# Keys' inverse norms, low-rank and weighing products, and the low halves at a seam of the expert passes

## The reference, cut to what matters

```
p    = h @ w_in                          # f, v/g, nine feature tiles (rw), then q, k, v of the window attention
kk   = k * kk_scale ; kk = kk / max(norm(kk over the 64 of a head), 1e-12)
w, a = sigmoid(w0 + w_up(tanh(..))), sigmoid(a0 + a_up(..))     # "low-rank", two directions
out  = scores @ v  for the gated linear attention, rms-normed and gated         # "weighing"
```

## Time and profile before

| | |
|---|---|
| median of 3 runs | 2022.44 us (2021.68 to 2023.82) |
| time of the profiled execution | 2018.09 us |
| its span, first to last instruction | 2016.3 us |
| mean granted clock of TensorE | 0.97 |
| TensorE busy | 1830.6 us, 91% |
| VectorE busy | 1610.4 us, 80% |
| ScalarE busy | 1090.9 us, 54% |
| GpSimd busy | 145.0 us, 7% |

### The profile page before, as it was taken

One profiled execution on the slowest core, in us unless ns is written; L12 is line 12 of the kernel. 1 busy time (PEld: TensorE's weight loads), 2 busy tenths in 40 slices (PEclk: granted clock), 3 DMA queues, 4 the chain that ended last, 5 costly groups with the idle time before them and its releaser, 6 DMA issues. The chain is left out here.

```text
span 2016.3 us, 31666 instructions
## 1 busy us (share of the span) xinstructions
PE 1830.6 (91%) x12866; PEld 1562.5 (77%) x12866; DVE 1610.4 (80%) x2113; ACT 1090.9 (54%) x1316; POOL 145.0 (7%) x151
## 2 busy tenths in 40 slices
PE   2989989998989989999899968997999999999998
PEld 2876769997866769997777657876788788787886
DVE  6778888987788888987579487557888888988887
ACT  2643636653653637562565333125677677776775
POOL 0000000000000000000056047300000000000000
PEclk9989999999999999999999987998899999999999
DMA  7667766656567757556522100006599899898997
GB/s 282 208 222 242 256 226 252 233 205 225 198 217 244 260 189 289 219 196 242 182 83 64 61 12 15 19 16 247 191 372 375 316 377 375 318 373 316 349 381 292
DMA packets 158288, 460.54 MB, mean 228 GB/s; under 512 B 11072, under 2 KB 13760, under 8 KB 155584
## 3 DMA queue, kind: packets, MB, share of 16 engines
q1 hardware_dynamic: 158144, 458.52, 63.7%
HBM read 457.43 MB, written 1.05 MB: 227 GB/s over the span
## 5 line engine op out<-in xcount | busy, mean ns | idle before, releaser
L217 DVE TENSOR_TENSOR me_wlow<-me_w,me_whigh 128x2048 fp32r<-128x2048 f32 (+1 forms) x203 | 451.5, 2247 | 77.5 <-ACT me_whigh L212 77.1
L212 ACT ACTIVATE me_whigh<-me_w 128x2048 fp32r<-128x2048 f32 (+1 forms) x203 | 380.3, 1885 | 116.9 <-PE ps L225 107.2
L223 PE MATMUL ps<-me_whigh,me_xhigh 128*128 128x512 f32 x512 | 204.0, 398 | 5.1 <-PEq L124 3.1
L225 PE MATMUL ps<-me_whigh,me_xlow 128*128 128x512 f32 x528 | 206.9, 392 | 0.0
L223 PE MATMUL ps<-up_xhigh,ffn_whigh 128*128 128x256 f32 x704 | 199.8, 284 | 2.6 <-DVE ffn_wlow L217 1.5
L224 PE MATMUL ps<-me_wlow,me_xhigh 128*128 128x512 f32 x512 | 200.5, 392 | 0.0
L224 PE MATMUL ps<-up_xlow,ffn_whigh 128*128 128x256 f32 x704 | 199.2, 283 | 0.0
L225 PE MATMUL ps<-up_xhigh,ffn_wlow 128*128 128x256 f32 x704 | 199.2, 283 | 0.0
L217 DVE TENSOR_TENSOR ffn_wlow<-ffn_w,ffn_whigh 128x2048 fp32r<-128x2048 f32 (+1 forms) x72 | 149.3, 2110 | 42.4 <-ACT ffn_whigh L212 42.3
L217 DVE TENSOR_TENSOR mix_wlow<-mix_w,mix_whigh 128x1024 fp32r<-128x1024 f32 (+2 forms) x116 | 140.0, 1210 | 21.8 <-ACT mix_whigh L212 21.7
L212 ACT ACTIVATE ffn_whigh<-ffn_w 128x2048 fp32r<-128x2048 f32 (+1 forms) x72 | 123.2, 1760 | 43.1 <-PE ps L225 43.1
(11 more groups left out here) (682 smaller groups left out, 4147.8 us busy)
## 6 DMA issues: line engine op xcount, KB each, us to landing
me_w<-w_exp_gate SPq DMA_DIRECT2D x34, 2048.0 KB, 9.8
me_w<-w_exp_up SPq DMA_DIRECT2D x34, 2048.0 KB, 10.3
me_w<-w_exp_down SPq DMA_DIRECT2D x32, 2048.0 KB, 10.4
mix_w<-w_mix SPq DMA_DIRECT2D x108, 512.0 KB, 4.0
mix_ada_w<-ada_w SPq DMA_DIRECT2D x96, 512.0 KB, 4.6
ffn_w<-ffn_w_up SPq DMA_DIRECT2D x20, 2048.0 KB, 7.8
ffn_w<-ffn_w_down SPq DMA_DIRECT2D x8, 2048.0 KB, 8.8
sec_w<-w_in SPq DMA_DIRECT2D x31, 512.0 KB, 3.6
```

Of the source, the lines that this page charges most:

```text
L212: return nc.scalar.activation(high, x, ACT.Copy)
L217: return nc.vector.tensor_tensor(low, x, high.bitcast(F32), ALU.subtract)
L223: nc.tensor.matmul(out, lh, rh, start=start, stop=False)
L225: return nc.tensor.matmul(out, ll, rh, start=False, stop=stop)
```

## The change

1. The squares of the scaled keys are made on ScalarE (generator `norms_act`, planned at 89.9), the sums over a head on TensorE ahead of `nq` 0, in two outputs `kn` that are new in the list `names`. ScalarE copies them out (108.5) and takes the root (126.0). VectorE makes the maximum and the reciprocal at t_weigh + 0.1. Later two instructions make the scaled and normed keys in one go. The old squares, sums, roots, maximum, reciprocal and product at the old places go.
2. On VectorE the scans of direction 0 are planned at t_weigh + 1.25, those of direction 1 at + 4.0, and the keys of direction 1 move from + 5.6 to + 10.3.
3. On TensorE the low-rank products are planned 0.8 earlier and the weighing products 0.8 earlier, which puts all ten ahead of piece `nk` 2 (130.9). The gate products stay at 131.8, behind it.
4. In `passes` the number of low halves made ahead at a start (`made`) and left at an end (`left`) are arguments. Each pass leaves one low half instead of three; the loop's pass starts with one and makes halves 1 and 2 itself, half 1 ahead of `gated_sum` and half 2 behind it.

```diff
--- before.py
+++ after.py
@@ -2256,6 +2256,8 @@
             if name in ("f", "rw"):
                 names.append((name, i))
             elif i == 0:
+                if name == "nq":
+                    names += [("kn", 0), ("kn", 1)]
                 names += [(name, t) for t in tiles[name]]
         units = Units(core, sem, "sec", 4, names)
         done, part_done = pieces.done, sem("sec_part_done")
@@ -2340,6 +2342,11 @@
         def products(pe):
             for p, (name, i, _, n) in enumerate(pieces.rows):
                 yield pieces.at[p]
+                if (name, i) == ("nq", 0):
+                    for hp in range(2):
+                        pe.wait_ge(kk_squared, hp + 1)
+                        nc.tensor.matmul(units.open(pe, ("kn", hp)), consts["head_ones"], key_sq[:, hp],
+                                         start=True, stop=True).then_inc(kk_summed, 1)
                 pieces.arrived(pe, p)
                 if p == 0:
                     pe.wait_ge(x_lows[1], 1)
@@ -2410,9 +2417,10 @@
 
         kk, kn, sw, sa, kt, rt, k2, up, tot, gt = (keys[n] for n in ("kk", "kn", "sw", "sa", "kt", "rt", "k2", "up", "tot", "gt"))
         up_here, low, low_read, gate_read = sem("up_here"), sem("low"), sem("low_read"), sem("gate_read")
-        kk_own, kk_summed, kk_rooted, scanned, key_own, key_exp, key_done, key_pool = (sem(n) for n in (
-            "kk_own", "kk_summed", "kk_rooted", "scanned", "key_own", "key_exp", "key_done", "key_pool"))
-        logs_made, keys_made = (3, 7), 10
+        kk_squared, kk_summed, kk_rooted, scanned, key_own, key_exp, key_done, key_pool = (sem(n) for n in (
+            "kk_squared", "kk_summed", "kk_rooted", "scanned", "key_own", "key_exp", "key_done", "key_pool"))
+        keys_made, logs_made = 4, (7, 11)
+        key_sq = ycat[:, :, A_W:A_W + NTOK]
 
         def low_bank(i):
             return core.ps[:, 6 + i % 2, :]
@@ -2420,7 +2428,7 @@
         def low_pe(pe):
             for i in range(8):
                 which, d, hp = i // 4, (i // 2) % 2, i % 2
-                yield t_low[i]
+                yield t_low[i] - 0.8
                 pe.wait_ge(up_here, 16)
                 pe.wait_ge(copied[1], len(SPANS))
                 pe.wait_ge(mixed, 1)
@@ -2436,11 +2444,21 @@
                 pe.wait_ge(low_read, 7 + t)
                 nc.tensor.matmul(low_bank(t)[:, 0:A_W], X[:, 8, (2 + t) * P:(3 + t) * P], up[:, 2 * A_W:], start=True, stop=True)\
                     .then_inc(low, 1)
+
+        def norms_act(act):
             for hp in range(2):
-                yield t_weigh + 5.7 + 0.05 * hp
-                pe.wait_ge(kk_own, 4)
-                pe.wait_ge(gate_read, hp + 1)
-                nc.tensor.matmul(low_bank(hp), consts["head_ones"], kn[:, hp], start=True, stop=True).then_inc(kk_summed, 1)
+                yield ready_at(("rw", 3)) + 3.4 + 0.1 * hp
+                units.read(act, ("rw", 2 + hp))
+                nc.scalar.activation(key_sq[:, hp], X[:, 2 + hp, :], ACT.Square, scale=fv["kk_scale"][:, hp:hp + 1])\
+                    .then_inc(kk_squared, 1)
+            for hp in range(2):
+                yield pieces.when("nq", 0) + 1.0 + 0.1 * hp
+                act.wait_ge(kk_summed, hp + 1)
+                units.close(nc.scalar.activation(key_sq[:, hp], units.bank(("kn", hp)), ACT.Copy), ("kn", hp))
+            for hp in range(2):
+                yield when(len(SPANS), 2.3 + 0.1 * hp)
+                units.read(act, ("kn", hp))
+                nc.scalar.activation(key_sq[:, hp], key_sq[:, hp], ACT.Sqrt).then_inc(kk_rooted, 1)
 
         def low_act(act):
             for i in range(8):
@@ -2453,10 +2471,6 @@
                 yield t_weigh + 1.5 + 0.05 * t
                 act.wait_ge(low, 9 + t)
                 nc.scalar.activation(gt[:, t, :], low_bank(t)[:, 0:A_W], ACT.Copy).then_inc(gate_read, 1)
-            for hp in range(2):
-                yield t_weigh + 6.0 + 0.05 * hp
-                act.wait_ge(kk_summed, hp + 1)
-                nc.scalar.activation(kn[:, hp], low_bank(hp), ACT.Sqrt).then_inc(kk_rooted, 1)
             for d in range(2):
                 yield t_weigh + 7.5 + 2.0 * d
                 act.wait_ge(key_own, logs_made[d])
@@ -2473,27 +2487,36 @@
                 own += 1
                 ins.then_inc(key_own, 1)
 
-            for hp in range(2):
-                yield t_weigh + 1.3 + 0.1 * hp
-                dve.wait_ge(weighed, TT)
-                units.read(dve, ("rw", 2 + hp))
-                V.tensor_scalar(kk[:, hp], X[:, 2 + hp, :], fv["kk_scale"][:, hp:hp + 1], None, ALU.mult).then_inc(kk_own, 1)
-                dve.wait_ge(kk_own, 2 * hp + 1)
-                V.tensor_tensor(kn[:, hp], kk[:, hp], kk[:, hp], ALU.mult).then_inc(kk_own, 1)
+            yield t_weigh + 0.1
+            dve.wait_ge(kk_rooted, 2)
+            mine(V.tensor_scalar(key_sq, key_sq, 1e-12, None, ALU.max))
+            dve.wait_ge(key_own, own)
+            mine(V.reciprocal(key_sq, key_sq))
             for d in range(2):
                 for hp in range(2):
-                    yield t_weigh + 3.6 + 0.4 * d + 0.2 * hp
+                    yield t_weigh + (1.25, 4.0)[d] + 0.2 * hp
                     dve.wait_ge(low_read, 2 * d + hp + 1)
-                    dve.wait_ge(out_own, 6)
+                    if d == 0:
+                        dve.wait_ge(weighed, TT)
+                    else:
+                        dve.wait_ge(out_own, 6)
                     V.tensor_tensor_scan((rt, k2)[d][:, d, hp], consts["chunk_start"], sw[:, d, hp], 0.0, ALU.mult, ALU.add)\
                         .then_inc(scanned, 1)
+            yield t_weigh + 4.5
+            dve.wait_ge(key_own, own)
+            dve.wait_ge(weighed, TT)
+            for hp in range(2):
+                units.read(dve, ("rw", 2 + hp))
+                mine(V.scalar_tensor_tensor(out=kk[:, hp], in0=X[:, 2 + hp, :], scalar=fv["kk_scale"][:, hp:hp + 1],
+                                            in1=key_sq[:, hp], op0=ALU.mult, op1=ALU.mult))
+            assert own == keys_made
             for d in range(2):
                 c = [a[:, d].rearrange("p h t -> p (h t)").rearrange("p (c n) -> p c n", n=RW_CHUNK) for a in (kt, k2, rt, sw)]
                 kt_, k2_, rt_, l_ = c
                 sums = (rt_, k2_)[d]
                 end = sums[:, :, RW_CHUNK - 1:RW_CHUNK]
                 ends = end.to_broadcast([P, 16, RW_CHUNK])
-                yield t_weigh + 4.6 + 1.0 * d
+                yield t_weigh + (4.6, 10.3)[d]
                 dve.wait_ge(scanned, 2 * d + 2)
                 mine(V.tensor_copy(tot[:, d].rearrange("p h c -> p (h c)"), end.squeeze(2)))
                 if d == 0:
@@ -2505,15 +2528,6 @@
                     mine(V.tensor_tensor(rt_, kt_, l_, ALU.add))
                     mine(V.tensor_tensor(k2_, k2_, l_, ALU.subtract))
                 assert own == logs_made[d]
-            yield t_weigh + 10.5
-            dve.wait_ge(kk_rooted, 2)
-            mine(V.tensor_scalar(kn, kn, 1e-12, None, ALU.max))
-            dve.wait_ge(key_own, own)
-            mine(V.reciprocal(kn, kn))
-            yield t_weigh + 11.0
-            dve.wait_ge(key_own, own)
-            mine(V.tensor_tensor(kk, kk, kn, ALU.mult))
-            assert own == keys_made
             for d in range(2):
                 yield t_weigh + 16.0 + 6.0 * d
                 dve.wait_ge(key_own, own)
@@ -2692,7 +2706,7 @@
                                             mm.then_inc(multiplied[s], 1)
                             mm.then_inc(multiplied[s], 1)
             for t in range(TT):
-                yield t_weigh + 0.2 + 0.2 * t
+                yield t_weigh - 0.6 + 0.2 * t
                 pe.wait_ge(copied[0], len(SPANS) + 1)
                 pe.wait_ge(copied[1], len(SPANS))
                 for i in range(NT4):
@@ -2873,7 +2887,7 @@
             @block.scalar
             def _(act):
                 in_turn(arrived(act), final_act(act), norms[1][2](act), context_act(act), pieces.high_parts(nc, act), bound_act(act), gate_act(act),
-                        values_act(act), levels_act(act), shift_act(act), bent_act(act),
+                        values_act(act), levels_act(act), shift_act(act), bent_act(act), norms_act(act),
                         attended_reads(nc.scalar, act, 1), low_act(act))
 
             @block.gpsimd
@@ -4209,7 +4223,7 @@
              "me_back", "me_added", "me_pick_turned", "me_pick_copied", "me_key_here", "me_picked", "me_gathered",
              "me_token_high", "me_token_low", "me_sum_high", "me_sum_low", "me_next0", "me_next1")
 
-    def passes(n_tiles, slots_of, groups_of):
+    def passes(n_tiles, slots_of, groups_of, made, left):
 
         with core.stage(*names) as (
                 block, high, low, half_done, silu, hid_done, hid_turned, hid_high, hid_low, summed, back, added,
@@ -4228,11 +4242,11 @@
                     if t and u % len(plan) == RAW:
                         sp.wait_ge(picked, t)
```

(23 more changed lines are left out.)

## The result

Measured beside each other, the kernel before takes 2022.3 us (2015.98 to 2027.41, 20 runs) and the changed one 2038.23 us (2021.79 to 2050.33, 20 runs): ratio 1.0068, 95% interval 1.0052 to 1.0084. It is slower, as forecast, but by 15.9 us instead of 4.1, outside the range of 2017.5 to 2031. The runs also scatter over 28.5 us where those of before scatter over 11.4. The profiled execution is the longest of the 20: span 2048.5 us, mean granted clock 0.951.

A forecast was written before the change was run, and what follows sets the result against it. TensorE was taken to bound the projection stage early, VectorE's and ScalarE's order late. Stage +7.2 us (8.5 - 2.9 + 1.6) and passes -3.1 gave +4.1, forecasting 2026.5 us, range 2017.5 to 2031.

The forecast's parts named there:

- The step that failed: Projection stage, TensorE: the ten low-rank and weighing products ahead of `nk` 2 start at 1127.1 and take 15.2 us.
- The three signs: Prediction wrong if TensorE's stop in `nv` 0 is under 4 us, the bank wait absent, or passes end as late.
- Sums on TensorE: Sums over a head, moved ahead of `nq` 0 with no wait behind them, add 1.8 us on TensorE.
- Bank wait: Within `nq` 0, TensorE's tile 3 waits for feature tile 8's bank to be closed: +2.0 us, bounds 0 to 2.3.
- Wait for the far copy: Ahead of the ten thin products, TensorE stands still 1.1 us while ScalarE copies the far scores.
- GpSimd's hold: GpSimd's first key product holds VectorE's low half of `nv` 1: +1.0 us, between 0 and 2.3.
- TensorE's stop in `nv` 0: TensorE idles 7 to 8 us within `nv` 0, awaiting ScalarE's late read; the lower clock behind it adds 1.6 us.
- The gates behind `nk` 2: Gate products staying behind `nk` 2 make ScalarE's second gate copy, then the root for the weighed values, 3.8 us later.
- The passes: Ends of the two expert passes: each 1.6 us sooner, less 0.1 for a tight meeting, -3.1 us in all.
- A: Rival, about even: GpSimd, bank-wait and `nv` 0 clock terms fall low, +0.8 us, 2023.2; chance 0.35.
- B: Rival, faster: an earlier high half of `nv` 1 lets VectorE's relief count, -2.1 us, -4.1 without bank wait; chance 0.22.
- C: Slower, the prediction's own sum: 2026.5 us, upper end 2029.6 if the passes give nothing; chance 0.43.

The follow-up runs named there:

- e5: The changed kernel run once more, unaltered, on the chip of the other experiments: 2032.41 us against 2022.61 for the kernel before.
- e7: Changed kernel with the ten thin products behind `nk` 2 again and direction 1's keys before the low half of `nv` 1: 2024.88 us against 2022.61 for before.
- e8: Changed kernel with the two gate products also ahead of `nk` 2: 2030.39 us against 2022.61 for the kernel before.
- e4: Changed kernel with the keys of direction 1 ahead of the low half of `nv` 1 again: 2025.85 us against 2024.57 for before.
- e3: Kernel before with only the change at the ends of the expert passes: 2021.17 us against 2024.57 for before.
- e6: Changed kernel with the ends of the expert passes as before: 2033.55 us against 2022.61 for the kernel before.
- e9: Changed kernel with six products of `nk` 2 run in the stop ahead of the ten thin products: 2027.25 us against 2024.78 for before.
- e10: Kernel before with ScalarE's far-scores copy held until `nk` 2 is multiplied, adding a stop ahead of the ten thin products: 2034.05 us against 2024.78.
- e2: Kernel before with only the low-rank and weighing products moved ahead of `nk` 2: 2026.33 us against 2024.57 for before.
- e11: Kernel before with the passes' change, and ScalarE's `nk` reads and high half of `nv` 1 ahead of direction 0's exponentials: 2019.63 us against 2024.78.

## Why the prediction was wrong

The sign and the order held; a term that I had written down as certain did not.

**The step that failed** is "The ten products start at 1127.1 and take 1143.70 - 1128.49 = 15.2 us". It took their length from rows at full clock and carried it over to a place where the step itself puts 1.1 us of idle time ahead of them. In part of the executions (4 of 7 profiles with such a stop) they then run at 1.2 GHz: 26.0 us in the changed kernel's profile. `nk` 2 behind them begins slow too, 1162.1 to 1169.4 = 7.3 us instead of 5.7. Together 12.4 us, and against e5's execution the stage from the far scores on is 86.5 - 73.8 = 12.7 us longer. I had given the clock a term only in `nv` 0 and at the passes, and from "as behind 1.96 us at 1163.80" took it that short stops are safe. That row shows dense products behind a stop, not thin ones, and the same trace of before has a stop with the other outcome, which the prediction passed over (TensorE's timeline and a window of before):

```profile
1155.21 0.76 PE L223 MATMUL ps<-sec_whigh,sec_xhigh 128*128 128x512 f32 x1 [2.79 <-DVE sec_wlow L217]
...
1155.00:1158.00 3.00, 2.79 (x6) 1.79 (x6) 3.00 (x6) 0.46 (x1) 0.00 (x0) 0.54 0.00 0
```

The three signs by which the prediction wanted to know itself wrong (no long stop in `nv` 0, no bank wait, late ends of the passes) did not come, since none of them looked at the ten products.

**The order** was right in the main. In e5, without the slow ten, the stage is 112.1 - 102.6 = 9.5 us longer, predicted 7.2; 4.7 of it lie ahead of the far scores. From the far scores to the end it is 73.8 - 69.1 = +4.7, predicted 7.2 - 3.1 = +4.1. By its points:

- Sums on TensorE: 1.98 us at 1102.73, predicted 1.8.
- Bank wait: predicted 2.0 within 0 to 2.3. Measured 0.58 to 0.60 in six profiles, 3.46 in e5, 3.44 in e7, none over 0.5 in e8. It depends on how far TensorE is ahead of VectorE when it gets there. The clock behind the wait of 3 us was 1.00 in e5 and e7 and 0.59 to 0.74 in the others, and with it at 1.00 GpSimd comes early and holds VectorE up, where the prediction had it start later and VectorE 0.3 us sooner. The upper bound was too low. The far scores start 1.8 us late in the changed kernel's profile and 4.7 in e5 (predicted 3.1).
- Wait for the far copy: 1.20, predicted 1.1. As a length it was right, and it was taken for all that a stop costs.
- VectorE's wait for the root: 7.75 us, predicted over 5; ahead of the low half of `nv` 1: 3.60, predicted 3.6.
- GpSimd's hold: the low half took 2.14 us instead of 1.20, so 0.94, predicted 1.0. GpSimd's product ran from 1184.08 to 1186.45, and the low half, begun at 1185.40, ended 1.1 us behind it. The Trainium skill's page "SBUF — State Buffer", section "SBUF: two separate sides", says that a VectorE instruction with two inputs in SBUF is blocked for the whole of a GpSimd instruction that began before it and reads SBUF; the trace agrees.
- TensorE's stop in `nv` 0: predicted one of 7 to 8 us. It came as two, 4.44 and 6.42, with six products at 1.2 GHz between them (clock 0.50 from 1184.5 to 1190). The kernel before has two there as well, 2.08 and 1.96 us, of which the prediction read one. My 1.6 us for the clock there is too small: behind `nk` 2 the products that follow each other 0.3 to 0.6 us apart instead of 0.23 cost 1.6 us in before, 4.0 in the changed kernel's profile and 4.5 in e5, so 2.4 to 2.8 more. e4 undoes the later stop, and its stage from the far scores on is 69.3 us, 4.5 less than e5's.
- No wait ahead of `nv` 3: as predicted.
- The gates behind `nk` 2: by e8's profile they were worth 5.8 us of stage, the 3.8 of the root among it; its runs do not resolve a gain.
- The passes: 3.1 predicted; 3.4 by the medians of e3, 1.6 each in the profile. The clock stayed at the first, and then TensorE waited 1.23 us at 1903.39 for VectorE's low half of a sum, as the prediction had it; the runs can't tell 0.3 us.

**The sum again**, with what was measured. Both profiles of the changed products with the slow ten (after, e6) have a stage of 121.8 us, +19.2; less 3.4 for the passes that is +15.8. e5's stage of +9.5 makes +6.1, and with the short bank wait an execution without the slow ten would be at 1.8 + 4.7 - 3.4 = +3.1, an estimate, since no profile of this kernel shows that pair. So without the slow ten the time is inside the predicted range. The median of 20 runs at +15.9 lies at the value with them, e5's at +9.8 between. So the size of the median depends on how often the clock falls, and this was not alike in the two sets of runs.

**The rivals.** A and B counted on the bounded terms and on an earlier high half; both asked for a clock that stays. C was right in sign, and its upper end of 2029.6 fell short since no case of mine had the clock fall in the thin products. Two bounds did not follow from the working: B with its bank term sums to 2018.3, not 2017.5, and C's own range began at 2024.5, where A still claimed all up to 2026.4. The range lacked a case for it altogether; a bound would have been the ten products at half clock, up to another 15.2 us.

**Left open:** what makes the clock fall in one execution and stay in the next. The page "TensorE: Matmul & The Clock Gate" of the Trainium skill, section "What's actually happening", says that the gate goes by TensorE's recent activity and is not in step with the kernel. The traces agree as far as one program gave both kinds, but no run here set the moment at which the row meets the gate, so this was not shown. That the stop is what makes it possible is shown by e9 and e10. How often it happens differs: e2 has the same stop, fast products in its profile and a median only 1.8 us above before, and nothing here says why.

## What to carry to other kernels

Where a row of thin products moves, price it at both clocks, and look at what stands right ahead of it: ahead of dense products a stop cost little (1.96 us kept the clock, 2.79 us cost 1.1 us in the products behind), and one of 1.2 us ahead of thin ones can cost 11 us. Here six dense products put into the stop took the loss away. When runs scatter more after an edit than before, compare two profiles of the same program before explaining either. Work taken from an engine shows in the time only where that engine ends the wait: the norms' move cost time in e7, and only with ScalarE's reads ahead of its exponentials did a profile show a shorter stage (99.7 us against e11's 102.4), which the runs did not confirm.

## What the runs showed of the hardware

- After 1.20 to 1.24 us of idle time, and 2 us or more of work at full clock behind it, TensorE's granted clock fell to 0.50 while it was working without a break on thin float32 products (64 columns, or 64 rows), in four of seven profiles, and stayed there for over 20 us of such work; it rose again in the dense products behind (0.86 over 1162.0 to 1175.9). Behind dense products without a stop the same row kept 1.00 in all seven profiles.
- The same program with the same stop did both: 15.2 and 26.0 us for the same ten products.
- So it was behind the wait of 3 us (2.97 and 3.00 us): over the products between the two groups of line 2678 the clock was 1.00 in e5 and 0.62 in the changed kernel's first profile.
- A product of 512 columns in the fast 32-bit format takes 0.23 us from start to start at full clock and 0.43 at half; a weighing group took 3.79 us and 7.09, the last four low-rank products 3.94 and 6.69.
